# The chunked delta rule by pairs of heads instead of by chunks, in a two-model transformer kernel

## The chip, the cores and the metric

The kernel runs on one core of one Trainium2 chip. The metric is the device time of one launch in microseconds (us).

## The reference, cut to what matters

Two models run one after the other on 512 tokens of width 1024, each two layers deep, all in float32. The change touches only the mixer of the second model, which runs once in each of its two layers. One projection gives 19 ranges of 128 columns, and one of 286 that is kept by token. Nine of the 19 (q, k and v of six heads of width 64) pass a causal convolution of four taps and silu. Then comes the gated delta rule in chunks of 64 tokens:

```python
q = l2norm(q) * D ** -0.5;  k = l2norm(k)
g = jnp.cumsum(g, axis=-1)                       # inside each chunk of 64
decay = exp(where(incl, g[..., :, None] - g[..., None, :], -inf))
lower = where(strict, (k * beta) @ k.T * decay, 0)
u, w = split(triangular_solve(I + lower, [v * beta, k * beta * exp(g)]))
attn = q @ k.T * decay

def step(state, xs):                             # 8 steps, one a chunk
    v_new = u_i - w_i @ state
    o_i = (q_i * exp(g_i)) @ state + a_i @ v_new
    state = state * exp(g_last) + (k_i * exp(g_last - g_i)).T @ v_new
```

Seven further ranges (three of queries, four of keys and values of a sparse attention) are used by the attention that follows. Six of them are rotated by position first. The last three are the gate z of the delta rule.

## The kernel before

The second model's mixer, `second_mixer`, has two regions with a barrier of all engines between them. The first, in which the change lies, holds the norm of the input, the projection, the delta rule and the rotation. The second, `attention_region`, holds the attentions.

Within a region each helper (`items_lane`, `key_norm_lane`, `delta_lane`, `rotary_lane`) writes a program for every engine as a generator that yields planned times. `weave` sorts the programs of one engine by these times and issues them in that order. So the planned times fix nothing but the order of instructions on each engine. An engine that reaches a wait stops there with all that stands behind it.

The projection goes by items of 128 columns. One item is eight pieces of three matmuls (`three_products`, L493 to L495), as its operands are split in a high and a low half. Its weights are split by ScalarE (L479) and VectorE (L484) while three items of them fit in the buffers. A convolution item leaves its bank through one ScalarE copy (L765) and three VectorE operations (L794, L796, L798), then silu (L769). Four row items come first, then 19 of 128 columns: nine convolution items, three of z, three of queries, four of keys and values.

`key_norm_lane` normalises all six tiles of q and k when all convolution items are through. It starts with an explicit load of ScalarE's table set that holds both exp and ln, as `inverse_root` takes Ln (L549) and then Exp (L551).

`delta_lane` then makes four rounds, one for each 128 tokens. A round treats two chunks of 64 of all six heads. It computes decays (L3333, L3334), transposes k and v (L3336, L3338), and makes the two triangular matrices (`low`, `low_t`, L3495 to L3509 on VectorE). A block inverse takes five levels, each with a product L3373, a ScalarE copy L3466, products L3385 and L3390 and a VectorE subtraction L3524, twice over (`b` = 0, 1: the head of a pair). Then come u and w (L3399, L3404), two steps of the recurrence (L3417, L3422, L3429 on TensorE, L3535 and L3545 on VectorE) and the output (L3437, L3473, L3552). GpSimd makes masks and masked parts. Pieces of the last ten items are planned between these products.

`rotary_lane` is planned behind the last item: six products L3571, each with a GpSimd product (L3586) and two VectorE operations (L3595, L3598), then four products L3579 with copies L3605.

Of the kernel before, what the change touches and what calls it, by code (L numbers as in the profile page):

```python
# [17 lines left out]
P = 128  # L18
# [4 lines left out]
ALU = mybir.AluOpType  # L23
# [147 lines left out]
def second_constants():  # L171
# [5 lines left out]
    c["causal_row"] = np.concatenate([np.zeros((P, S - P)), causal], axis=1)  # L177
    c["strict_row"] = np.concatenate([np.where(i[None, :] <= i[:, None], NEG, 0.0), np.zeros((P, S - P))], axis=1)
# [442 lines left out]
class Item:  # L621


    def __init__(self, kind, load, at, width, out, chunks=(), scale=None, tile=0, func=None, moving=None, ready=(), each=()):
        self.kind, self.load, self.at, self.width, self.out = kind, load, at, width, out
        self.chunks, self.scale, self.tile, self.func, self.moving, self.ready, self.each = chunks, scale, tile, func, moving, ready, each
        self.begin, self.length = 0.0, 0.0
# [7 lines left out]
def items_lane(k, r, lane, w, ranges, items, h_ready, ring, w_hi, w_lo, banks, tap=None, bias=None, quick=False):  # L635
# [108 lines left out]
    def _(act):  # L744
        steps = [(split_time(part), 0, part) for part in range(len(parts))]
        for m, item in enumerate(items):
            end = item.begin + item.length
            if item.kind == "conv":
                steps += [(end, 2, m), (end + 3.0, 3, m)]
# [1999 lines left out]
def sparse_lane(k, r, lane, nq, ks2, kw2, vs_rows, vw_rows, cmp_out, gates, mixT, tile_out):  # L2749
# [67 lines left out]
    def _(dve):  # L2817
        def maxima(p):
            for u in range(2):
# [4 lines left out]
                nc.vector.tensor_tensor_reduce(probs[:, n % DEEP, 0:width(p)], logits[:, u, 0:width(p)], k.at["causal_row"][:, S - width(p):S],  # L2824
# [57 lines left out]
def stick_lane(k, r, lane, sq, sk, sv_rows, mixT, head_out, banks, out_ps, space, items_out, pairs_done, bank_free):  # L2882
# [62 lines left out]
    def _(dve):  # L2945
        def masked(n):
            for b in range(TC):
# [4 lines left out]
                nc.vector.tensor_tensor(z[:, n % 2, AT[b]:AT[b + 1]], banks[:, b % 2, 0:WIDTH[b]], k.at["strict_row"][:, 0:WIDTH[b]],  # L2952
# [102 lines left out]
def attention_region(k, a, l, tiles, nq, kc2, vc2, ks2, kw2, vs_rows, vw_rows, gates, sq, sk, sv_rows, gz, mixT):  # L3055
# [3 lines left out]
    with Region(k) as r:  # L3059
# [8 lines left out]
        kc_dup, vc_rows = r.sbuf("kc_dup", [P, 2 * N_CMP]), r.sbuf("vc_rows", [P, 2, HD])  # L3068

# [117 lines left out]
def key_norm_lane(k, r, lane, tiles, silu_done, sq, rstd, stat):  # L3187

    nc = k.nc
    (squared, stat_done, log_done, rstd_done, normed) = r.semaphores("qk", "squared stat_done log_done rstd_done normed")  # L3190
    N = len(tiles)

    @lane.vector
    def _(dve):
        for j in range(N + 1):
            yield j / (N + 1)
            if j < N:
                dve.wait_ge(silu_done, j + 1)
                if j >= 2:
                    dve.wait_ge(stat_done, j - 1)  # L3200
                nc.vector.tensor_tensor(sq[:, j % 2, :], tiles[j][0], tiles[j][0], ALU.mult).then_inc(squared, 1)
            yield (j + 0.5) / (N + 1)
            if j:
                x, scale = tiles[j - 1]
                dve.wait_ge(rstd_done, j)
                nc.vector.scalar_tensor_tensor(x, x, scale, rstd[:, (j - 1) % 2, :], ALU.mult, ALU.mult).then_inc(normed, 1)

    @lane.tensor
    def _(pe):
        for j in range(N):  # L3210
            yield (j + 0.1) / (N + 1)
            pe.wait_ge(squared, j + 1)
            if j >= 2:
                pe.wait_ge(rstd_done, j - 1)
            nc.tensor.matmul(stat[:, j % 2, :], k.at["ones_64"], sq[:, j % 2, :], start=True, stop=True).then_inc(stat_done, 1)

    @lane.scalar
    def _(act):
        nc.scalar.preload_act_table_set(EXP_LN_SET)
        for j in range(N):  # L3220
            yield (j + 0.5) / (N + 1)
            act.wait_ge(stat_done, j + 1)
            if j >= 2:
                act.wait_ge(normed, j - 1)
            inverse_root(k, act, rstd[:, j % 2, :], rstd[:, j % 2, :], stat[:, j % 2, :], 1.0, log_done, j + 1).then_inc(rstd_done, 1)

    return normed


def delta_lane(k, r, lane, qkv, g, beta, beta_eg, to_end, mixT, scratch, state, banks, steps_ready, normed, silu_done, ROUND):  # L3230

    nc = k.nc
    H, T, LEVELS = N_GDN, GDN_T, 5
    N = H * HD
    (zeroed, prepared, turn_done, decay_done, exp_done, run_done, rows_done, run_out, masked, tb_done, qrun_done, kk_done, kq_done,
     low_done, low_t_done, attn_done, first_done, inv_done, part_done, y_done, y_out, t_done, uw_done, uw_out, new_done, new_out,
     inter_done, grow_done, state_done, intra_done, inter_out, pass_out) = r.semaphores(
        "delta", "zeroed prepared turn_done decay_done exp_done run_done rows_done run_out masked tb_done qrun_done kk_done kq_done "
        "low_done low_t_done attn_done first_done inv_done part_done y_done y_out t_done uw_done uw_out new_done new_out "
        "inter_done grow_done state_done intra_done inter_out pass_out")  # L3240

    def pieces(first, count):
        return [scratch(first + i) for i in range(count)]

    def by_head(x):
        return x.rearrange("p (b t n) -> p b t n", b=2, t=T)

    v_beta, k_beta, k_end, q_run, run, attn_t, y_sb = pieces(0, 7)
    lows, invs = scratch(7, 2), scratch(9, 2)
    low, low_t = lows[:, 0:N], lows[:, N:2 * N]  # L3250
    inv, inv_t = invs[:, 0:N], invs[:, N:2 * N]
# [744 lines left out]
```

## Time and profile before

| what | us |
|---|---|
| median of three runs (lowest to highest) | 3831.06 (3827.61 to 3834.22) |
| the profiled execution, its own time | 3828.58 |
| its span | 3826.8 |
| TensorE busy in the span | 3475.4 (91%) |
| VectorE busy | 1780.1 (47%) |
| ScalarE busy | 1308.2 (34%) |
| GpSimd busy | 420.6 (11%) |
| mean granted TensorE clock | 0.949 of full |
| first region, layer 0, first convolution item to the last VectorE instruction | 1844.87 to 2094.1 |

A busy TensorE is not one at its peak: ends of matmuls are modelled, and a busy share holds stretches at the lower clock. The region stands in the trace twice, once for each layer, with nearly the same rows. Times of rows count from the start of the span.

### The profile page before, as it was taken

The page shows a single profiled execution, that of the slowest core. Times are in us where ns is not written, and L with a number is a line of the kernel's source. Part 1 is how long each engine was busy: PE and PEld are TensorE (multiplying, and loading weights), DVE is VectorE, ACT ScalarE, POOL GpSimd, SP SyncE. Part 2 cuts the span into 40 slices and gives each one's busy share as a digit, 9 for nine tenths or more (in the row PEclk, how much of TensorE's full clock was granted, in tenths as well). Part 3 has the DMA queues.
Part 4 walks back from the last instruction along what each step waited for, and adds up shares of the span by engine and source line. Part 5 has one row for each costly group of instructions (what it writes and reads, how often), then busy time and mean ns, then how long its engine had stood idle before and what let it go on. Part 6 is the DMA issues. An engine that isn't in the chain of part 4 may idle for free. (4 is left out here: it accounts for less than half of the span.)

```text
span 3826.8 us, 46458 instructions
## 1 busy us (share of the span) xinstructions
PE 3475.4 (91%) x19317; PEld 2705.3 (71%) x19317; DVE 1780.1 (47%) x2762; ACT 1308.2 (34%) x2038; POOL 420.6 (11%) x351
## 2 busy tenths in 40 slices
PE   5989897999999789998897988999989988899998
PEld 4877765788777567886665756788766665577886
DVE  4775465443332534332544454444444444554534
ACT  2332353223232332322422353333333134533333
POOL 0001000120000101100023000221001310013100
PEclk7999998999999899999899999999989989999999
DMA  6651215333221032331301103232122020213231
GB/s 228 199 175 45 78 34 187 118 124 110 90 75 55 1 132 69 105 109 35 99 18 27 37 1 110 87 100 101 66 76 61 2 63 1 88 55 110 77 110 50
DMA packets 230575, 316.69 MB, mean 83 GB/s; under 512 B 13133, under 2 KB 167606, under 8 KB 229086
## 3 DMA queue, kind: packets, MB, share of 16 engines
q1 hardware_dynamic: 230366, 313.72, 24.9%
q8 instruction: 154, 2.52, 0.3%
q14 instruction: 55, 0.45, 0.0%
HBM read 311.04 MB, written 6.85 MB: 83 GB/s over the span
## 5 line engine op out<-in xcount | busy, mean ns | idle before, releaser
L493 PE MATMUL out<-h_lo,w_hi 128*128 128x512 f32 x2608 | 1043.1, 400 | 52.1 <-DVE w_lo L484 47.8
L494 PE MATMUL out<-h_hi,w_hi 128*128 128x512 f32 x2608 | 1022.2, 392 | 0.0
L495 PE MATMUL out<-h_hi,w_lo 128*128 128x512 f32 x2608 | 1021.6, 392 | 0.0
L484 DVE TENSOR_TENSOR w_lo<-ring,w_hi 128x1024 fp32r<-128x1024 f32 (+2 forms) x459 | 560.7, 1227 | 980.0 <-ACT w_hi L479 974.9
L479 ACT ACTIVATE w_hi<-ring 128x1024 fp32r<-128x1024 f32 (+2 forms) x459 | 469.2, 1027 | 1152.9 <-PE out L495 1061.1
L493 PEld LDWEIGHTS out<-h_lo,w_hi 128*128 128x128 f32 x2608 | 494.0, 189 | 178.1 <-issue 60.4
L494 PEld LDWEIGHTS out<-h_hi,w_hi 128*128 128x128 f32 x2608 | 493.8, 189 | 111.9 <-issue 11.0
L495 PEld LDWEIGHTS out<-h_hi,w_lo 128*128 128x128 f32 x2608 | 493.6, 189 | 103.9
L493 PE MATMUL item_banks<-h_lo,w_hi 128*128 128x512 f32 (+1 forms) x632 | 289.4, 458 | 14.3 <-DVE w_lo L484 5.1
L494 PE MATMUL item_banks<-h_hi,w_hi 128*128 128x512 f32 (+1 forms) x632 | 255.1, 404 | 0.0
L495 PE MATMUL item_banks<-h_hi,w_lo 128*128 128x512 f32 (+1 forms) x632 | 254.8, 403 | 0.0
L493 PEld LDWEIGHTS item_banks<-h_lo,w_hi 128*128 128x128 f32 (+1 forms) x632 | 121.9, 193 | 55.4 <-issue 22.0
L493 PE MATMUL item_banks<-w_lo,h_hi 128*128 128x256 f32 (+1 forms) x320 | 104.7, 327 | 43.5 <-DVE w_lo L484 27.3
L495 PEld LDWEIGHTS item_banks<-h_hi,w_lo 128*128 128x128 f32 (+1 forms) x632 | 121.6, 192 | 31.0
L494 PEld LDWEIGHTS item_banks<-h_hi,w_hi 128*128 128x128 f32 (+1 forms) x632 | 122.4, 194 | 28.4 <-issue 8.2
L1503 POOL TENSOR_TENSOR tiles<-temp 128x512 f32<-128x512 f32 x44 | 72.8, 1655 | 568.8 <-DVE temp L1489 324.9
L428 DVE SCALAR_TENSOR_TENSOR tiles<-tiles,c_act 128x1024 f32<-128x1024 f32 x70 | 95.9, 1369 | 57.5 <-DMA tiles<-in_mod_w 56.3
L2264 POOL TENSOR_TENSOR tiles<-tiles 128x512 f32<-128x512 f32 x64 | 76.8, 1205 | 309.3 <-ACT tiles L2250 282.2
L1635 POOL TENSOR_TENSOR xT<-xT,tiles 128x512 f32<-128x512 f32 x20 | 30.2, 1537 | 709.8 <-DVE tiles L1624 709.8
L493 PEld LDWEIGHTS item_banks<-w_lo,h_hi 128*128 128x128 f32 x320 | 65.9, 206 | 57.7 <-DVE w_lo L484 27.9
L484 DVE TENSOR_TENSOR h_lo<-tiles,h_hi 128x2048 fp32r<-128x2048 f32 (+2 forms) x43 | 83.5, 1944 | 35.6 <-ACT h_hi L479 35.6
L494 PE MATMUL item_banks<-w_hi,h_hi 128*128 128x256 f32 (+1 forms) x320 | 96.8, 302 | 0.0
(499 smaller groups left out, 4635.8 us busy)
## 6 DMA issues: line engine op xcount, KB each, us to landing
ring<-in_mlp_w SPq DMA_DIRECT2D x30, 2048.0 KB, 8.5
ring<-in_w_up SPq DMA_DIRECT2D x44, 1024.0 KB, 7.4
tiles<-in_mod_w SPq DMA_DIRECT2D x80, 512.0 KB, 4.6
ring<-in_e_w_in SPq DMA_DIRECT2D x48, 512.0 KB, 4.1
ring<-in_w_down SPq DMA_DIRECT2D x10, 2048.0 KB, 7.7
ring<-in_w_in SPq DMA_DIRECT2D x16, 1024.0 KB, 5.2
ring<-in_o_w_in SPq DMA_DIRECT2D x7, 2048.0 KB, 7.9
tiles<-in_mod_w SPq DMA_DIRECT2D x8, 1024.0 KB, 8.8
```

Of the source, the lines that this page charges most:

```text
L428: nc.vector.scalar_tensor_tensor(total, slot, gain_of(c), total, ALU.mult, ALU.add).then_inc(summed, 1)
L479: return nc.scalar.activation(hi.bitcast(F32R), x, ACT.Copy)
L484: return nc.vector.tensor_tensor(lo.bitcast(F32R), x, hi, ALU.subtract)
L493: nc.tensor.matmul(out, wh, xl, start=start, stop=False, **kw)
L494: nc.tensor.matmul(out, wh, xh, start=False, stop=False, **kw)
L495: return nc.tensor.matmul(out, wl, xh, start=False, stop=stop, **kw)
L1503: nc.gpsimd.tensor_tensor(finish_dst(b.nth, j), acc[:, b.nth % 2, j, :], acc[:, b.nth % 2, 2 + j, :], ALU.mult).then_inc(finished, 1)
L1635: nc.gpsimd.tensor_tensor(k.xT[:, f, :], k.xT[:, f, :], temp[:, f, :], ALU.add).then_inc(pool_added, 1)
L2264: after=lambda j: nc.gpsimd.tensor_tensor(dst(j), dst(j), dst(j), ALU.mult))
```

## The change

The delta rule goes by pair of heads (three of them, `t`), with all four 128-token chunks at once. The tiles of one pair are 512 columns wide, where those of one round were 384 wide. The eight steps of the recurrence of pair t are planned beside the inverse of pair t+1. The states of all steps are kept (`hist`), so the products of q with the states are made together at the end of a pair. Items are reordered to q, k, v of pair 0, then pair 1, pair 2, then queries, keys and values, and z last. Each load of weights is now two transfers of 128 columns where it was one of 256. The silus of a pair stand together. The norms move into `delta_lane`, one pair at a time, and the explicit table load goes. The rotation stands behind the last item on the banks of the items, and waits for the output of pair 1. Two constants are merged into one, and three buffers of the attention are allocated later.

```diff
-        ranges += [[(W_GDN + t * 2 * P, 2 * P)] for t in range(2 * GDN_T)]
+        tile_of = [part * GDN_T + t for t in range(GDN_T) for part in range(3)]
+        cols_of = [W_GDN + j * P for j in tile_of] + [W_NQ + j * P for j in range(NSA_T)] + [W_KC, W_KC + P, W_KC + 2 * P, W_KW]
+        cols_of += [W_GDN + (3 * GDN_T + j) * P for j in range(GDN_T)]
+        ranges += [[(col, P) for col in cols_of[n:n + 2]] for n in range(0, len(cols_of), 2)]
...
-        BEGIN, DELTA, ROUND = 18.0, 94.0, 28.0
-            item.begin, item.length = at, 3.2 if item.load == 0 else 5.6 if at < DELTA else 9.4
+        BEGIN, PAIR, BESIDE = 18.0, 37.0, 7.0
+            item.begin, item.length = at, 3.2 if item.load == 0 else 5.6 if m < TC + 3 else BESIDE
+            items[TC + n].silu_at = last.begin + last.length + 2.0 + 0.7 * (n % 3)
+            here = items[TC + 2].silu_at + 8.5 + PAIR * t
+            pairs_at.append((here - 6.5 if t == 0 else here - 10.0, here, here + 36.0))
...
-        nc.scalar.preload_act_table_set(EXP_LN_SET)
...
+    def recurrence(pe, t, at):
...
+        for s in range(STEPS):
+            if s:
+                yield at + 2.6 * s
+                pe.wait_ge(state_done, (STEPS - 1) * t + s)
+                for b in range(2):
+                    last = nc.tensor.matmul((R0, R1)[b][rows, 0:HD], w_t[rows_of(b), (i * TC + c) * HD:(i * TC + c + 1) * HD], hist[rows_of(b), s, :],
+                                            start=True, stop=True)
+                last.then_inc(new_done, 1)
+            if s < STEPS - 1:
+                yield at + 2.6 * s + 1.3
+                if s:
+                    pe.wait_ge(new_out, (STEPS - 1) * t + s)
+                for b in range(2):
+                    last = nc.tensor.matmul(R0[rows_of(b), HD:2 * HD], of_head(k_end, b, c)[rows, :], of_head(u, b, c)[rows, :], start=True, stop=True)
+                last.then_inc(grow_done, 1)
...
+    def act_steps():
+            steps += [(norm_at + 1.3 + 1.3 * j, "norm", t, j) for j in range(2)]
+            steps += [(at + 1.5, "decay", t, 0), (at + 4.3, "run", t, 0), (at + 34.8, "uw", t, 0), (run_at + 2.6 * (STEPS - 1) + 1.6, "inter", t, 0)]
+            steps += [(at + 12.0 + 4.4 * n + 1.1 * b, "y", t, 2 * n + b) for n in range(LEVELS) for b in range(2)]
...
+    def dve_steps():
+            steps += [(at + 2.0, "rows", t, 0), (at + 4.2, "both", t, 0), (at + 6.0, "low", t, 0), (at + 8.5, "attn", t, 0)]
+            steps += [(at + 14.0 + 4.4 * n + 1.1 * b, "inv", t, 2 * n + b) for n in range(LEVELS) for b in range(2)]
+            steps += [(run_at + 2.6 * s + 0.7, "new", t, s) for s in range(1, STEPS)]
+            steps += [(run_at + 2.6 * s + 2.0, "state", t, s) for s in range(STEPS - 1)]
```

On TensorE a pair is planned as: decays at `at`, transposes +0.8, running sums +3.0, k times k (kk) +5.0, k times q (kq) +7.0, level n at +11.0 + 4.4n, u and w (uw) at +34.0.

## Rows read from the trace of the kernel before

**Rows 1.** The page's busy time of TensorE over the span.

```profile
PE 3475.4 (91%) x19317; PEld 2705.3 (71%) x19317; DVE 1780.1 (47%) x2762; ACT 1308.2 (34%) x2038; POOL 420.6 (11%) x351
```

**Rows 2.** Busy time by stretches of the first region, layer 0.

```profile
core 0: us, PE busy (x) PEld busy (x) DVE busy (x) ACT busy (x) POOL busy (x), PEclk, DMA share, GB/s
1845.00:1926.00 81.00, 74.43 (x290) 56.41 (x291) 44.95 (x58) 36.04 (x53) 4.67 (x5) 0.94 0.26 78
1926.00:1972.50 46.50, 43.46 (x625) 32.20 (x625) 19.41 (x39) 9.60 (x20) 13.21 (x15) 0.96 0.12 36
1972.50:2018.00 45.50, 42.63 (x620) 32.22 (x619) 17.73 (x37) 9.13 (x20) 13.18 (x15) 0.92 0.01 2
2059.20:2094.10 34.90, 27.87 (x554) 21.42 (x554) 15.79 (x36) 8.32 (x20) 9.75 (x11) 0.89 0.01 2
```

**Rows 3.** TensorE's waits, 1844 to 2037.4: us in total, times, longest.

```profile
PE delta_banks L3373 <- DVE delta_scratch L3509: 6.1, 3, 2.9
PE stat_banks L3215 <- DVE tiles L3201: 4.4, 2, 3.5
PE delta_banks L3333 <- DVE gdn_qkv L3206: 2.1, 1, 2.1
```

**Rows 4.** Timeline of TensorE, round 0: start, us, instructions.

```profile
1951.26 0.52 PE L3385 MATMUL delta_banks<-delta_scratch 64*64 64x64 f32 x12
1951.61 0.52 PE L3390 MATMUL delta_banks<-delta_scratch 64*64 64x64 f32 x12
...
1957.15 0.50 PE L493 MATMUL item_banks<-h_lo,w_hi 128*128 128x512 f32 x1
...
1958.05 0.56 PE L3373 MATMUL delta_banks<-delta_scratch,tiles 64*64 64x64 f32 x12
1958.54 0.50 PE L493 MATMUL item_banks<-h_lo,w_hi 128*128 128x512 f32 x1
```

**Rows 5.** Timeline of TensorE, items alone: two pieces in a row.

```profile
1855.13 0.40 PE L493 MATMUL item_banks<-h_lo,w_hi 128*128 128x512 f32 x1
...
1855.83 0.40 PE L493 MATMUL item_banks<-h_lo,w_hi 128*128 128x512 f32 x1
```

**Rows 6.** Timeline of VectorE: first and behind the last of the triangular block.

```profile
1936.78 0.61 DVE L3495 TENSOR_TENSOR delta_scratch<-delta_scratch,delta_banks 128x192 f32<-128x192 f32 x2
...
1940.90 0.61 DVE L3516 TENSOR_TENSOR delta_scratch<-delta_scratch,delta_banks 128x192 f32<-128x192 f32 x2
```

**Rows 7.** Timeline of VectorE at the end of a convolution item.

```profile
1898.05 0.75 DVE L794 SCALAR_TENSOR_TENSOR gdn_qkv<-item_banks,vec,gdn_qkv 128x511 f32<-128x511 f32 x1 [1.91 <-ACT gdn_qkv L765]
...
1900.51 1.22 DVE L484 TENSOR_TENSOR w_lo<-ring,w_hi 128x1024 fp32r<-128x1024 f32 x1
```

**Rows 8.** Timeline of ScalarE at the start of the norms.

```profile
1901.05 1.28 ACT L3219 ACT_TABLE_LOAD   x1
1903.56 0.69 ACT L549 ACTIVATE tiles<-stat_banks,const_sb 128x512 f32<-128x512 f32 x1 [1.22 <-PE stat_banks L3215]
```

**Rows 9.** Timeline of ScalarE in the first model: Exp, Ln, Exp.

```profile
122.64 1.28 ACT L844 ACT_TABLE_LOAD   x1
...
130.36 1.28 ACT L849 ACT_TABLE_LOAD   x1
131.65 0.26 ACT L849 ACTIVATE scan_scratch<-scan_scratch 128x64 f32<-128x64 f32 x1
131.93 1.28 ACT L853 ACT_TABLE_LOAD   x1
```

**Rows 10.** Timeline of TensorE: last item matmul, last two recurrence steps.

```profile
2037.07 0.40 PE L495 MATMUL item_banks<-h_hi,w_lo 128*128 128x512 f32 x1
...
2087.59 0.50 PE L3417 MATMUL delta_banks<-gdn_state,delta_scratch 64*64 64x64 f32 x9 [1.00 <-ACT delta_scratch L3470]
...
2088.87 0.56 PE L3429 MATMUL delta_banks<-delta_scratch 64*64 64x64 f32 x12 [0.37 <-DVE delta_scratch L3535]
2090.20 0.58 PE L3417 MATMUL delta_banks<-gdn_state,delta_scratch 64*64 64x64 f32 x6 [0.77 <-DVE gdn_state L3545]
```

**Rows 11.** Timeline of VectorE: a rotation's sum, and the region's last work.

```profile
2042.53 0.69 DVE L3598 TENSOR_TENSOR tiles<-tiles 128x512 f32<-128x512 f32 x1 [0.73 <-POOL tiles L3586]
...
2093.50 0.62 DVE L3552 TENSOR_TENSOR tiles<-tiles,delta_banks 128x192 f32<-128x192 f32 x2
```

More of the change, by code:

```diff
@@ L748, in _ @@
             if item.kind == "conv":
-                steps += [(end, 2, m), (end + 3.0, 3, m)]
+                steps += [(end, 2, m), (end + 3.0 if item.silu_at is None else item.silu_at, 3, m)]
             elif owner(m) == "act":
@@ L3193, in _ @@
     @lane.vector
     def _(dve):
[L3195 to L3218, printed above, removed]
-        nc.scalar.preload_act_table_set(EXP_LN_SET)
[L3220 to L3225, printed above, removed]
@@ L3633, in second_mixer @@
+        ranges += [[(col, P) for col in cols_of[n:n + 2]] for n in range(0, len(cols_of), 2)]
         items = [Item("rows", 0, 0, 2 * P + 30, by_token[:, c:c + 1, :], (c,)) for c in range(TC)]
-        items += [Item("conv", 1 + j // 2, j % 2 * P, P, qkv[:, j, :], tile=j) for j in range(3 * GDN_T)]
-        items += [Item("feat", 1 + j // 2, j % 2 * P, P, gz[:, j - 3 * GDN_T, :]) for j in range(3 * GDN_T, 4 * GDN_T)]
-        items += [Item("feat", 7 + j // 2, j % 2 * P, P, nq[:, j, :], scale=HD ** -0.5) for j in range(NSA_T)]
@@ L3637, in second_mixer @@
-        items += [Item("feat", 8, P, P, kv[:, 0, :]), Item("feat", 9, 0, P, kv[:, 1, :]), Item("feat", 9, P, P, kv[:, 2, :]),
-                  Item("feat", 10, 0, P, kv[:, 3, :])]
-        last_kv = len(items)
-        BEGIN, DELTA, ROUND = 18.0, 94.0, 28.0
+        outs = [qkv[:, j, :] for j in tile_of] + [nq[:, j, :] for j in range(NSA_T)] + [kv[:, j, :] for j in range(4)] + [gz[:, j, :] for j in range(GDN_T)]
+        last_kv = TC + 3 * GDN_T + NSA_T + 4
+        for n, out in enumerate(outs):
+            if n < 3 * GDN_T:
+                items.append(Item("conv", 1 + n // 2, n % 2 * P, P, out, tile=n))
+            else:
+                items.append(Item("feat", 1 + n // 2, n % 2 * P, P, out, scale=HD ** -0.5 if n < 3 * GDN_T + NSA_T else None))
@@ L3641, in second_mixer @@
+        BEGIN, PAIR, BESIDE = 18.0, 37.0, 7.0
         at = BEGIN
-        for item in items:
-            item.begin, item.length = at, 3.2 if item.load == 0 else 5.6 if at < DELTA else 9.4
+        for m, item in enumerate(items):
+            item.begin, item.length = at, 3.2 if item.load == 0 else 5.6 if m < TC + 3 else BESIDE
             at += item.length
+        for n in range(3 * GDN_T):
+            last = items[TC + 3 * (n // 3) + 2]
+            items[TC + n].silu_at = last.begin + last.length + 2.0 + 0.7 * (n % 3)
@@ L3646, in second_mixer @@
+        pairs_at = []
+        for t in range(GDN_T):
+            here = items[TC + 2].silu_at + 8.5 + PAIR * t
+            pairs_at.append((here - 6.5 if t == 0 else here - 10.0, here, here + 36.0))
         with mixing as r:
-            scratch_own = r.sbuf("delta_scratch", [P, 11 * N_GDN * HD])
+            scratch_own = r.sbuf("delta_scratch", [P, 12 * S])
             scratch_mix = mixT[:, GDN_T:DT, :].rearrange("p f n -> p (f n)")
-            state = r.sbuf("gdn_state", [P, GDN_T, HD])
+            hist, ends = r.sbuf("gdn_hist", [P, 2 * TC, HD]), r.sbuf("gdn_ends", [P, 2, 2 * TC])
@@ L3655, in scratch @@
             def scratch(first, count=1):
-                width = N_GDN * HD
-                if first < 11:
-                    return scratch_own[:, first * width:(first + count) * width]
-                return scratch_mix[:, (first - 11) * width:(first - 11 + count) * width]
+                if first < 12:
+                    return scratch_own[:, first * S:(first + count) * S]
+                return scratch_mix[:, (first - 12) * S:(first - 12 + count) * S]
             tables = r.lane(30.0, 0.0)
```

688 lines of the change are left out of this document (363 added, 325 removed).

## The prediction

> **What bounds the kernel now.** I read the page first. TensorE is busy in 91% of the span [rows 1]. So what another engine saves is worth only what TensorE waits for it. The change lies in one region, which stands in the trace twice, and I read its stretches next. In layer 0 it runs from the first convolution item at 1844.87 to the last VectorE work at 2094.1, so 249.2 us. TensorE is nearly full there until the last item ends, and less so at the end: 27.9 of the last 34.9 us [rows 2].
>
> The region splits at the last item matmul, which ends near 2037.4 [rows 10]. The first part takes 192.5 us and the tail 56.7 us. For the first part I rebuild the sum from prices. A piece of an item takes 0.70 us when pieces follow each other [rows 5], so 19 items of eight pieces are 106.4. Twelve small delta records start 0.35 us behind the twelve before them [rows 4]. A round has 528 such records, at most 15.4 us by this price, and some 3 us of wide products. By their starts in the same view a round is 17 us. Two and a half rounds lie before the last item ends, 42.2. Six norm products are 5.1. Next comes a cost of switching. A piece that stands alone between delta groups takes 0.90 us, and a lone group of twelve 0.49 [rows 4]. So each change from items to delta work and back costs 0.20 + 0.14 = 0.34 us. The timeline has 46 such pieces or runs of pieces, 15.6 us. The waits are 13.0: three for the triangular block, two in the norms, one in front of the first round, and 0.4 of others [rows 3]. The granted clock was 0.94, 0.96 and 0.92 in three stretches [rows 2], each a mean of time at 2.4 GHz and some at 1.2 GHz, which loses 4.9 + 1.9 + 3.6 = 10.4. The sum is 192.7, against 192.5 measured. So this account can be used on the changed order.
>
> **The content does not change.** Five levels of four rounds of three pairs are five levels of three pairs of four chunks. Only six products for each of the first or last steps fall away. The same matmuls, masks and copies are done in wider pieces. VectorE and ScalarE save some fixed time, but neither is the bound [rows 1]. What changes is order.
>
> **The tail, a gain.** After the last item the changed TensorE program has one level and a half, u and w of pair 2, one recurrence and the whole rotation. A recurrence step now lasts 1.28 + 1.33 us without cover [rows 10], with 24 and 12 records and several VectorE operations in it. The changed step has four records and one VectorE operation on either side. Nothing shows it, so I bound it: it can't be longer than 2.6, and two lone matmuls of 0.27 us with two VectorE operations of about 0.3 give 1.15 at least. I take 1.3, near the lower end: seven steps, 9.1. The rotation stands beside them. A sum of it waits 0.73 us on VectorE for GpSimd's product [rows 11], and what stands behind it in VectorE's order, the recurrence's steps too, waits as well. Walking the orders from the last item gives 7 us to u and w, 4 to the first step, 13 for the steps with rotation between them (the 9.1, and 4 for four of its products at 1.0), and 3 for the outputs, 27. At 2.6 a step it would be 36. TensorE is half idle there. The clock stood at 0.89 in the present tail [rows 2], so I add 3. That makes 30 where 56.7 stood: 26.7 less.
>
> **The first part, work that moves in.** The tail keeps 280 small records (8.2 us) and the ten products of the rotation. All other delta work, 68 (four rounds) less 8.2, now lies before the last item ends, with items and norms 171.3 in all. It was 153.7, so 17.6 more.
>
> **Switching, a loss.** I sort the planned times of the diff. Sixteen items stand beside the pairs, one piece each 0.875 planned microseconds. A level has four groups spread over 4.4, and new and grow steps of the recurrence stand alone between them. So 84 groups of delta work stand between pieces where 46 stood. 38 more at 0.34 are 12.9 us.
>
> **Waits.** These I walk through, each from the place in the orders.
> - The triangular block held VectorE from 1936.78 to 1940.90, 4.1 us for 384 columns [rows 6]. For 512 it is 5.3. In pairs 1 and 2 the `low` step (at + 6.0) stands in VectorE's order 0.2 before the state of step 2 of the recurrence beside it. TensorE's next `new` product needs this state, and only two pieces, 1.6 us, stand between. So TensorE stands for 3.8 us, twice. Queued behind are kq and all items. Smaller ones of this kind (rows, weight splits and copies ahead of `new`) are 1.5 + 0.3 + 0.6. In pair 0 no recurrence stands beside it, and nine pieces cover the block: 0.6.
> - The end of a convolution item holds VectorE for three operations and a weight split, 1898.05 to 1901.7 [rows 7], 3.6 us. Before, all nine stood ahead of the delta rule. Now six stand beside pair 0. Nearly all are covered by two or three pieces, but the last stands in front of the subtraction that u and w need: 1.8.
> - The norms. The explicit load of ln with exp goes [rows 8]. In the first model, where none stands between, Exp, Ln and Exp each bring a load of 1.28 us [rows 9]. So each norm now brings a load for Ln and one for Exp, 12 a layer, and the silus of pairs 1 and 2 bring three more, where one stood: 14 more, 18 us of ScalarE. Most are hidden. In pair 0 the two norms take 6.5 us instead of 4, the next item's convolution sits on VectorE before the second, and the transposes of k wait 4.5 us where 0.7 would do. In pair 1 the loads add 1.0 in front of u and w, in pair 2 0.3.
>
> The sum is 7.6 + 2.4 + 0.6 + 1.8 + 4.5 + 1.3 = 18.2, against 13.0: 5.2 more. Three stand for about 4 us, and the present stretches with such waits lost 2 to 4 us of clock each [rows 2, 3]. I take 11 against 10.4.
>
> A row shows the load at 1.28 us with the next activation right behind it [rows 9]. The Trainium skill (ScalarE: Activation LUTs, What ACT_TABLE_LOAD costs) gives the same 1283 ns, but adds a drain of some 1380 ns to every switch, and its section on table sets says to batch calls by set, which speaks against this change. By that price the three waits at norms would be some 5 us a layer longer. The row shows no drain, so I leave it out.
>
> **At no cost.** The weights now come in two transfers of 128 columns. Each is asked for some three items (17 us) ahead of its use. Doubled transfers would have to take three times as long to show. GpSimd's wider masks run a level ahead. The merged constant and moved buffers cost nothing.
>
> **Sum.** For one layer 17.6 + 12.9 + 5.2 + 0.6 - 26.7 = 9.6 us more, for two 19. The profiled execution took 3828.6, 2.5 below the median, which is 3831.1. So 3850, and 0.5% slower. Own range of this case: switching 26 to 32, waits 14 to 24, clock 8 to 14, tail 28 to 36 a layer, not all at one end: 3838 to 3866.
>
> **Rivals.**
> - *Faster: TensorE doesn't stop.* If VectorE has the small recurrence steps through before the triangular block, and the norms keep ahead, waits are 5 instead of 18.2, and the clock loses 3 instead of 11. That is 21.2 less a layer: 11.6 faster than now, so 3808. Waits plus clock below 19.6 us a layer decide it. For it speaks that more pieces stand between the stages than now. Against it speaks that the block's place is fixed in the order. Chance 0.24.
> - *Even: the loads don't bite.* One set chosen for Ln and Exp, or norms that are early, take away 4.7 of waits and 2.5 of clock a layer: 2.4 slower a layer, 3836. Rows 9 speak against it. Chance 0.20.
> - *Much slower: the fine steps don't fit.* Beside levels, each of 28 recurrence hops waits another 0.4 us, as VectorE and ScalarE are caught by splits of weights: 11.2 more a layer, 3873. TensorE's present waits in steps are only 0.4 to 1.0 [rows 10], without cover. Chance 0.06.
>
> **Numbers.** The forecast's case has 0.50. What a measurement of this kernel can tell from no change is 0.2%, 7.7 us. Faster by more: 0.25, most of it the first rival. Within: 0.20. Slower: 0.55. Leaving out a tenth on each side, the range reaches from just above the first rival's value to the last one's: 3811 to 3868.
>
> **What would show it.** The last item matmul of layer 0 should end near 2074 to 2077 (content 171.3, switching 28.6, waits 18.2, clock 11 from 1844.87), and the region near 2104. The waits of TensorE should name the VectorE product into `hist` at 3 to 4 us, twice a layer, and the transposes of k in pair 0. ScalarE should have 14 more table loads a layer. Lone pieces should still take 0.90. I am wrong if the last item ends before 2065, if loads are few, or if the tail is over 40 us.

## The result, and the profile after

The changed kernel takes 3850.98 us, median of five runs (3847.08 to 3857.33), against 3831.06 before. The ratio is 1.0052, with a 95% interval of 1.0038 to 1.0066. The forecast was 3850, and "slower" its likeliest side. The sum came out right; two of its parts did not, and they cancelled.

The profiled run was the slowest of the five, 3857.3. At the first convolution item of layer 0 it was already 5.2 us behind (1850.11 against 1844.87), so I compare lengths from there. The page's busy times first:

```profile
PE 3511.2 (91%) x19257; PEld 2707.5 (70%) x19257; DVE 1779.7 (46%) x2718; ACT 1338.2 (35%) x2040; POOL 420.9 (11%) x309
```

They hardly differ from [rows 1]: 36 us more of TensorE and 30 of ScalarE, each about a hundredth of the span. What changed can be read only by place. Busy time by stretches of the changed region in layer 0, to be held against [rows 2]; its last item ends at 2072.1 and the next region's first product stands at 2109.6:

```profile
1850.00:1900.00 50.00, 48.78 (x285) 36.62 (x285) 34.01 (x47) 28.06 (x42) 15.87 (x12) 0.97 0.33 85
1900.00:1950.00 50.00, 46.33 (x587) 33.39 (x587) 23.18 (x31) 23.54 (x34) 8.36 (x8) 0.97 0.17 44
1950.00:2000.00 50.00, 46.33 (x632) 33.32 (x630) 22.28 (x39) 9.81 (x17) 16.43 (x12) 0.97 0.13 33
2000.00:2072.10 72.10, 65.37 (x801) 45.51 (x799) 26.62 (x47) 17.46 (x28) 13.53 (x9) 0.95 0.01 2
...
2072.10:2088.00 15.90, 13.68 (x233) 8.33 (x232) 10.28 (x18) 2.84 (x6) 8.85 (x6) 1.00 0.00 1
2088.00:2109.60 21.60, 16.67 (x116) 8.67 (x116) 4.39 (x15) 2.98 (x5) 0.00 (x0) 0.51 0.00 1
```

The reader is to see two things in the seventh column, the granted clock. In the first part it is 0.95 to 0.97, no worse than before. In the tail it is 1.00 up to 2088 and then 0.51, which is 1.2 GHz nearly throughout. Where it fell, TensorE runs a recurrence step, waits, and runs the next. That these waits bring the clock down is not shown by this row.

From the first convolution item to the last item's end the kernel before took 192.6 us in layer 0 and 189.6 in layer 1; after, 222.0 and 222.2. From there to the next region's first product it took 57.9 and 57.7, and now 37.5 and 37.4. So layer 0 loses 9.0 and layer 1 loses 12.3. The 3 us between them are the old kernel's: its first part lost 10.0 us to the clock in layer 0 and 6.8 in layer 1 (length times what the mean granted clock lacks to 1), with the same order and the same stops.

TensorE's waits in the first part of layer 0 (us in total, times, longest), which answer to [rows 3]:

```profile
PE stat_banks L3412 <- DVE gdn_hist L3582: 9.0, 2, 5.3
PE delta_banks L3381 <- ACT delta_scratch L3482: 4.0, 2, 2.6
PE item_banks L492 <- DVE w_lo L483: 2.6, 1, 2.6
PE delta_banks L3364 <- DVE delta_scratch L3563: 1.0, 1, 1.0
PE delta_banks L3325 <- DVE gdn_qkv L3518: 0.8, 1, 0.8
PE stat_banks L3313 <- DVE tiles L3514: 0.3, 1, 0.3
```

The first row is the predicted stop: the product `new` waits for the state in `hist`, once beside pair 1 (3.7 us) and once beside pair 2 (5.3). The third row stands ahead of the first convolution item, in both kernels. Without it the waits are 15.1; by the same count they were 13.1 before.

The timeline of VectorE shows the first of these stops from the inside:

```profile
1957.10 0.75 DVE L3538 TENSOR_TENSOR delta_scratch<-delta_scratch,delta_banks 128x256 f32<-128x256 f32 x2 [1.26 <-PE delta_banks L3343]
1957.77 0.75 DVE L3542 TENSOR_TENSOR delta_scratch<-delta_scratch,delta_banks 128x256 f32<-128x256 f32 x2
1958.55 1.75 DVE L3546 TENSOR_TENSOR delta_scratch<-delta_scratch,const_sb 128x1024 f32<-128x1024 f32 x1
1960.40 2.10 DVE L3549 TENSOR_TENSOR delta_scratch<-const_sb,delta_scratch 128x1024 f32<-128x1024 f32 x1
1962.42 0.27 DVE L3582 SCALAR_TENSOR_TENSOR gdn_hist<-gdn_hist,gdn_ends,stat_banks 128x64 f32<-128x64 f32 x1
```

And TensorE's timeline on the other side:

```profile
1957.85 0.33 PE L3420 MATMUL stat_banks<-delta_scratch,gdn_qkv 64*64 64x64 f32 x4
...
1962.74 0.37 PE L3412 MATMUL stat_banks<-gdn_hist,delta_scratch 64*64 64x64 f32 x2 [3.67 <-DVE gdn_hist L3582]
```

The operation that TensorE needs is 0.27 us long and could have started at 1958.2. It stands behind 5.3 us of the triangular block.

The second row of waits was not predicted at that place. ScalarE's timeline behind it:

```profile
1931.57 0.37 ACT L3482 ACTIVATE delta_scratch<-delta_banks 128x256 f32<-128x256 f32 x1
1931.95 1.28 ACT L548 ACT_TABLE_LOAD   x1
1933.24 0.69 ACT L548 ACTIVATE tiles<-stat_banks,const_sb 128x512 f32<-128x512 f32 x1
1933.95 1.28 ACT L550 ACT_TABLE_LOAD   x1
1935.24 0.63 ACT L550 ACTIVATE tiles<-tiles 128x512 f32<-128x512 f32 x1
1935.78 0.67 ACT L764 ACTIVATE gdn_qkv<-item_banks,vec 128x512 f32<-128x512 f32 x1
1936.35 1.05 ACT L478 ACTIVATE w_hi<-ring 128x1024 fp32r<-128x1024 f32 x1
1937.30 0.37 ACT L3482 ACTIVATE delta_scratch<-delta_banks 128x256 f32<-128x256 f32 x1
```

Between two copies of the last level stand one norm of the next pair with two table loads, a convolution's first tap and a weight split: 5.4 us. The region has 17 loads where it had 3, the 14 more that were forecast.

In the tail, TensorE's timeline: first a product of the rotation at the high clock with what follows it, then the recurrence of the last pair. The rotation has six products L3608 and four L3616, all of the same size.

```profile
2073.60 1.13 PE L3608 MATMUL item_banks<-tiles,const_sb 128*128 128x512 f32 x2
2074.65 0.68 PE L3376 MATMUL delta_banks<-delta_scratch 64*64 64x64 f32 x16
...
2086.12 0.33 PE L3412 MATMUL stat_banks<-gdn_hist,delta_scratch 64*64 64x64 f32 x4 [0.75 <-DVE gdn_hist L3582]
2086.84 0.33 PE L3420 MATMUL stat_banks<-delta_scratch,gdn_qkv 64*64 64x64 f32 x4 [0.39 <-DVE delta_scratch L3572]
...
2096.49 0.48 PE L3412 MATMUL stat_banks<-gdn_hist,delta_scratch 64*64 64x64 f32 x4
2097.35 0.48 PE L3420 MATMUL stat_banks<-delta_scratch,gdn_qkv 64*64 64x64 f32 x4 [0.38 <-DVE delta_scratch L3572]
2097.76 2.07 PE L3616 MATMUL item_banks<-tiles,const_sb 128*128 128x512 f32 x2
2099.76 0.48 PE L3412 MATMUL stat_banks<-gdn_hist,delta_scratch 64*64 64x64 f32 x4
```

I call it a hop from one product of four records, over VectorE's answer, to the next. A hop is 0.72 us at the high clock (2086.12 to 2086.84) and 0.86 at the low one (2096.49 to 2097.35). A product of the rotation costs 2.00 at the low clock (2097.76 to 2099.76) and 1.06 at the high one (2073.60 to 2074.65).

### The profile page after: what moved, and what is told of

Same layout as the page of the kernel before. It is cut to its first block and busy times, and to the rows that moved or that the text cites. A ratio compares the mean times of both kernels' runs of the same rounds, so it can differ in the third digit from the quotient of the medians.

```text
span 3855.6 us, 46228 instructions
## 1 busy us (share of the span) xinstructions
PE 3511.2 (91%) x19257; PEld 2707.5 (70%) x19257; DVE 1779.7 (46%) x2718; ACT 1338.2 (35%) x2040; POOL 420.9 (11%) x309
## 5 line engine op out<-in xcount | busy, mean ns | idle before, releaser
L492 PE MATMUL item_banks<-h_lo,w_hi 128*128 128x512 f32 (+1 forms) x632 | 299.6, 474 | 14.1 <-DVE w_lo L483 5.1
L492 PEld LDWEIGHTS item_banks<-h_lo,w_hi 128*128 128x128 f32 (+1 forms) x632 | 123.0, 195 | 57.7 <-issue 22.1
```

Of the source, the lines that this page charges most:

```text
L492: nc.tensor.matmul(out, wh, xl, start=start, stop=False, **kw)
```

## The experiments

In the code of an experiment a diff is against the changed kernel, if nothing else is said. The measured lengths are those of layer 0, layer 1 behind a stroke: first part (first convolution item to the end of the last) and tail (from there to the next region's first product). They come from one profiled execution of each kernel, the ratios from all that were timed. "Stops" are gaps of TensorE over 0.2 us in layer 0's first part, "groups" the groups of delta work that stand between pieces there. A ratio moves by a thousandth for 3.8 us, and its interval reaches 0.9 to 1.4 thousandths either way.

| kernel | ratio to before (95%) | first part | tail | stops | groups |
|---|---|---|---|---|---|
| before | 1 | 192.6 / 189.6 | 57.9 / 57.7 | 13.1 | 54 |
| changed | 1.0052 (1.0038 to 1.0066) | 222.0 / 222.2 | 37.5 / 37.4 | 15.1 | 90 |
| set | 1.0034 (1.0022 to 1.0047) | 218.7 / 217.4 | 37.6 / 37.6 | 12.2 | 90 |
| block in three | 1.0039 (1.0025 to 1.0053) | 219.4 / 218.1 | 37.6 / 37.6 | 13.9 | 90 |
| block in four | 1.0002 (0.9993 to 1.0011) | 214.5 / 214.6 | 34.0 / 33.9 | 9.5 | 90 |
| pieces in twos | 1.0004 (0.9995 to 1.0013) | 213.8 / 211.7 | 36.4 / 37.6 | 14.3 | 57 |
| items of 7.6 | 1.0079 (1.0065 to 1.0092) | 231.1 / 229.9 | 32.0 / 32.0 | 16.9 | 91 |
| no rotation | not measured | 222.0 / 223.8 | 26.0 / 25.4 | as changed | 90 |
| three edits | 0.9932 (0.9919 to 0.9944) | 198.9 / 197.6 | 37.6 / 37.6 | 4.8 | 57 |
| the same, in fours | 0.9932 (0.9919 to 0.9945) | 197.7 / 198.0 | 39.7 / 39.6 | 8.2 | 32 |
| the same, items of 6.6 | 0.9948 (0.9935 to 0.9962) | 199.6 / 198.3 | 40.4 / 40.9 | 10.4 | 55 |
| the same, items of 7.4 | 0.9976 (0.9968 to 0.9985) | 209.2 / 207.9 | 36.4 / 36.4 | 9.9 | 56 |
| the same, rotation early | 0.9919 (0.9906 to 0.9933) | 199.0 / 197.6 | 36.1 / 36.1 | 4.8 | 57 |
| before, in twos | 1.0022 (1.0012 to 1.0032) | 193.6 / 190.7 | 59.5 / 59.5 | 16.7 | 38 |

**The set.** Are the table loads in a place that counts?

```diff
+                if n == 0:
+                    nc.scalar.preload_act_table_set(EXP_LN_SET)
                 inverse_root(k, act, rstd[:, n, :], ...
...
```

> The changed kernel with one line more: ScalarE loads the set that holds ln and exp once ahead of each pair's two norms, so that Ln and Exp don't bring a load each. The changed kernel stands at 1.0052 of the one before. Theory (the loads are late in places that count: 2.65 and 1.37 us of TensorE's waits in front of the last level of pairs 0 and 1, 0.8 at the transposes of k, and about 2 us of clock behind them, a layer): 12 us less in all, a ratio near 1.002, table loads down from 58 to about 40, and these waits under 1 us. Rival (ScalarE is at 35%, the loads only fill its idle time, and the waits are those of the norms themselves): ratio 1.004 to 1.006 with as many fewer loads.

The loads fell from 58 to 40, and the two waits for ScalarE's copies (4.0 us) are gone. But 0.8 us came back in front of u and w and 0.4 at the transposes. The time is 1.8 thousandths lower, some 7 us of the 12 expected. The two intervals overlap, but the first part is shorter in both layers, by 3.3 and 4.8 us. So the loads do bite. The edit takes away nine of the 14 further loads a layer, and what the other five cost is not measured.

**The block in three.** Does VectorE's order make the stops at the state?

The block's six operations stay in their order, and stand under three names instead of one:

```diff
-            steps += [(at + 2.0, "rows", t, 0), (at + 4.2, "both", t, 0), (at + 6.0, "low", t, 0), (at + 8.5, "attn", t, 0)]
+            steps += [(at + 2.0, "rows", t, 0), (at + 4.2, "both", t, 0), (at + 6.0, "low_t", t, 0), (at + 6.3, "low", t, 0), (at + 7.6, "first", t, 0), (at + 8.5, "attn", t, 0)]
...
```

> The changed kernel with VectorE's triangular block in three steps instead of one (products for the transposed half, products for the other half, then the first level's two wide operations), so that the state and the new value of steps 2 and 3 of the recurrence beside it get in between. The same operations. Theory (VectorE's order makes the 3.67 and 5.29 us stalls of pairs 1 and 2): both fall below 1.5 us, with 2 us of clock that is 9 to 10 us a layer, 19 in all, a ratio near 1.000. Rival (the block is the chain itself: what doesn't wait at the recurrence waits at the first level for the block's end): the wait goes to the first level or to the product with the new value, and the ratio stays at 1.003 or above.

The gain is 1.3 thousandths, a quarter of the theory's, and the intervals overlap, so it is hardly clear of noise. The rows tell more. In pair 2 the stop of 5.3 became two of 0.7 and 1.6. In pair 1 it grew from 3.7 to 1.8 + 3.8. VectorE's timeline there says why:

```profile
1954.33 2.09 DVE L483 TENSOR_TENSOR w_lo<-ring,w_hi 128x1024 fp32r<-128x1024 f32 x1 [1.51 <-ACT w_hi L478]
1956.45 0.29 DVE L3574 TENSOR_TENSOR delta_scratch<-delta_scratch,stat_banks 64x128 f32<-64x128 f32 x1
1956.77 1.86 DVE L3548 TENSOR_TENSOR delta_scratch<-delta_scratch,const_sb 128x1024 f32<-128x1024 f32 x1
1958.74 2.10 DVE L3551 TENSOR_TENSOR delta_scratch<-const_sb,delta_scratch 128x1024 f32<-128x1024 f32 x1
1960.87 0.75 DVE L3558 TENSOR_TENSOR delta_scratch<-delta_scratch,delta_banks 128x256 f32<-128x256 f32 x2
1961.54 0.27 DVE L3584 SCALAR_TENSOR_TENSOR gdn_hist<-gdn_hist,gdn_ends,stat_banks 128x64 f32<-128x64 f32 x1
```

The new value now waits behind a weight split, and the state of the next step behind both wide operations. The stop had only moved one step on. That pointed to a cut between the wide ones.

**Pieces in twos.** Is the 0.34 us per change from items to delta work real?

```diff
-                    yield item.begin + item.length * f / DT
+                    yield item.begin + item.length * (f - f % item.group) / DT
...
+            item.group = 1 if m < TC + 3 else 2
```

> The changed kernel with the items' pieces planned in twos beside the delta rule, so that 55 groups of delta work a layer stand between pieces instead of 86. The same work on all engines. Theory (each change from items to delta work and back costs TensorE 0.34 us): 31 x 0.34 = 10.5 us a layer less, 2 of it lost again as groups get less fine cover, so 17 less in all, a ratio near 1.001; two pieces in a row should take 1.60 us where two lone ones take 1.80. Rival (the extra time of a lone piece is time in which TensorE would wait for the other engines anyway): the waits in front of the levels grow by as much, and the ratio is 1.004 or above.

4.8 thousandths, with 33 groups fewer and stops as before. The timeline shows two pieces, the first and the group behind the second, 1.58 us apart, where two lone ones take 1.80:

```profile
1910.09 0.50 PE L492 MATMUL item_banks<-h_lo,w_hi 128*128 128x512 f32 x1
...
1911.67 0.68 PE L3376 MATMUL delta_banks<-delta_scratch 64*64 64x64 f32 x16
```

In layer 0 the first part is 8.2 us shorter. Stops give 0.8 of it, and the clock took 2.2 (from its rows, 10.3 us lost against 8.1). So 9.6 us go to 33 groups, 0.29 each. In layer 1 the same sum gives 0.25. The rival, that this time would be waited anyway, falls.

**Items of 7.6.** Would cover for the last level shorten the tail?

```diff
-        BEGIN, PAIR, BESIDE = 18.0, 37.0, 7.0
+        BEGIN, PAIR, BESIDE = 18.0, 37.0, 7.6
```

> The changed kernel with one number changed: an item beside the pairs is planned for 7.6 instead of 7.0, so that the 16 items reach to the last recurrence, and only it and the rotation stand behind the last item. Theory (the tail of 36 us is long because the last level, u and w and the recurrence stand there without cover, at half clock): the tail falls to about 24 us, the first part grows by 4.4 of content and 1 of switching, 6 to 7 us a layer less, a ratio near 1.002. Rival (pieces planned further apart leave the earlier hops with less cover): the first part's waits grow by 6 us a layer or more, and the ratio is 1.005 or above.

The rival's time came out, and not its mechanism: the first part grew by 9.1 and the tail fell by 5.5 only, but stops grew by 1.8 where the rival wanted 6. What moved in is 206 small records (1762 against 1968 stand in the first part), 6.0 us at the price of [rows 4], where I had put 4.4. With the stops and a group more that is 8.1 of the 9.1. My 24 us for it was wrong: the last recurrence, with all ten products of the rotation beside it, takes 32 by itself, however much cover the last level has.

**Three edits**, the first and third of these, and the block cut in four:

```diff
-            steps += [(at + 2.0, "rows", t, 0), (at + 4.2, "both", t, 0), (at + 6.0, "low", t, 0), (at + 8.5, "attn", t, 0)]
+            steps += [(at + 2.0, "rows", t, 0), (at + 4.2, "both", t, 0), (at + 6.0, "low_t", t, 0), (at + 6.3, "low", t, 0), (at + 7.6, "first", t, 0), (at + 8.9, "minus", t, 0),
+                      (at + 9.0, "attn", t, 0)]
...
```

> Three edits together: pieces in twos, the ln and exp set loaded once a pair, and VectorE's triangular block in four steps, with the state of step 3 between its two wide operations. Theory (the gains are of different kinds and add up: the twos alone gave 4.8 thousandths, the set 1.8; and the block gives more than the 1.3 thousandths of the cut in three, as no more than 2 us of it now stand in front of a state): 0.9965, about 13 us under the kernel before. Rival (the split of w_lo, which stands in VectorE's order beside the block, takes the place of each wait taken away): 0.999 to 1.001, with the wait named on w_lo's neighbour, the new value.

Better than both kernels, and better than its own theory. The block cut alone, below, says where the theory was short: it gives 5.0 thousandths, and the theory had left about 2 for it. Its stretches, to be held against those above (its items end at 2044.0):

```profile
1845.00:1900.00 55.00, 53.78 (x376) 41.34 (x377) 38.07 (x50) 25.98 (x42) 19.90 (x14) 0.97 0.30 77
1900.00:1950.00 50.00, 48.55 (x616) 35.30 (x614) 26.63 (x41) 20.32 (x32) 10.21 (x9) 1.00 0.17 44
1950.00:2000.00 50.00, 48.77 (x714) 37.46 (x715) 21.28 (x35) 13.88 (x24) 12.35 (x9) 1.00 0.13 33
2000.00:2044.00 44.00, 42.88 (x597) 32.13 (x597) 19.32 (x38) 6.84 (x14) 12.01 (x8) 1.00 0.01 2
2044.00:2081.60 37.60, 30.40 (x348) 17.07 (x349) 14.66 (x32) 5.82 (x11) 8.89 (x7) 0.71 0.00 1
```

From 1900 on the clock is 1.00 as long as items last. The stops at the state are 1.4 us in place of 9.0, and VectorE's timeline shows the state between the wide operations:

```profile
1950.10 1.86 DVE L3551 TENSOR_TENSOR delta_scratch<-delta_scratch,const_sb 128x1024 f32<-128x1024 f32 x1
1951.98 0.28 DVE L3588 SCALAR_TENSOR_TENSOR gdn_hist<-gdn_hist,gdn_ends,stat_banks 128x64 f32<-128x64 f32 x1
1952.18 1.98 DVE L3555 TENSOR_TENSOR delta_scratch<-const_sb,delta_scratch 128x1024 f32<-128x1024 f32 x1
```

**The block in four alone**, to see whether it needs the other two:

> The changed kernel with nothing but VectorE's triangular block cut in four steps, the state of step 3 standing between its two wide operations. Theory (in the kernel with three edits the stops at the state fell from 9.0 to 1.4 us a layer, by this edit; what the twos add there is small): stops at the state and the new value under 4 us, the clock of 1950 to 2000 above 0.98, 8 to 10 us a layer less, ratio near 1.0005. Rival (the three edits work only together: with lone pieces a split of w_lo takes the place of the block again, as in the cut in three, 5.6 us in pair 1): ratio 1.003 or above.

It doesn't. The wait at the state fell to 1.6 us (1.8 more at the new value), and the ratio by 5.0 thousandths. With 1.8 for the set and 4.8 for the twos the single edits make 11.6, and together they measured 12.0. So each of the three pays without the others. One thing was off: the clock of 1950 to 2000 stayed at 0.97, and ScalarE's stops of 4.0 us are still there; it rose to 1.00 only behind 2000.

By place they add up less neatly. In the first part of layer 0 the single edits take 3.3, 8.2 and 7.5 us, 19.0 together, where the three at once take 23.1. The rest of the block's gain, 3.5 us a layer, stands in the tail, which TensorE runs in the same order as before the edit:

```profile
2056.90:2090.80 33.90, 26.73 (x348) 15.57 (x349) 14.66 (x32) 5.82 (x11) 8.84 (x7) 0.85 0.00 1
```

It has 0.85 of the clock there where the changed kernel has 0.72. With the three edits the tail is back at 37.6 us and 0.71. What sets the clock of the tail is not shown, and this profiled execution was 4.9 us below its kernel's median, so part of these 3.5 may be the execution and not the edit.

**In fours.**

```diff
-            item.group = 1 if m < TC + 3 else 2
+            item.group = 1 if m < TC + 3 else 4
```

> As the kernel with three edits, with the pieces in fours: 29 groups of delta work by the plan instead of 55. Theory (TensorE pays per change, by the step from ones to twos 0.22 to 0.29 us): 26 x 0.25 = 6.5 us a layer less than in twos, minus what waits grow; if these grow by 3, 0.9945. Rival (groups in fours leave hops of levels back to back, each waiting 0.5 to 1 us for ScalarE's or VectorE's answer, 20 of them and more): waits grow by 10 us a layer or more, and it is slower than in twos, 0.998 or above.

Neither came out: the ratio is that of twos. In layer 0 the first part is 1.2 us shorter. 48 small records (1.4 us) moved from it to the tail, stops grow by 3.4 and the clock takes 1.7 more, so 25 groups fewer bring about 5 us, 0.20 each. The tail takes 2.1 back. From twos to fours the two prices balance.

**Items of 6.6 and of 7.4** with the three edits:

> As the kernel with three edits, with 6.6 instead of 7.0 for an item: the items end 6.4 planned us earlier, and another level and a half stand in the tail, beside the rotation's products. Theory (7.6 instead of 7.0 moved 4.4 us of content and the cover of the rotation, and cost 9 in the first part for 5.5 in the tail; the rotation's products are better filler beside levels than beside the small steps at half clock): the first part 6 to 8 us shorter, the tail 4 longer, 2 to 4 us a layer less than with 7.0. Rival (levels without cover pay 0.5 to 1 us a hop at half clock): the tail grows by 8 or more, no gain or slower.

> As the kernel with three edits, with 7.4 instead of 7.0 for an item: the items reach to u and w of the last pair, and only the last recurrence, its outputs and the rotation stand behind. Theory (7.6 cost more than it gave because the first part grew by 9 where 4.4 moved in; the rest of it were switching and stops, which the three edits have made cheap): first part 5 to 6 longer, tail 5 shorter, within 0.1% of 7.0, 0.993. Rival (the tail is bound by the last recurrence and the rotation beside it, so that cover given to the last level is cover taken from nothing): slower by 3 us a layer or more, 0.9947 or above.

Both slower, the first by little: its interval overlaps that of 7.0, and its two parts together are 3.4 and 4.0 us longer a layer. With 6.6 a stop of 5.1 us stands in front of pair 0's first level. In VectorE's order a convolution item's three operations and a weight split (1893.74 to 1898.5) have come between the two wide operations that the cut had parted. At 7.0 no such stop is there. Taken off by subtraction it would leave 6.6 ahead by 1 to 2 us a layer; no run shows that. So this run tells of a collision, and leaves its theory open. With 7.4 the first part grows by 10.3, of which 5.1 are stops and 3.7 the 128 small records that moved in, and the tail falls by 1.2. Cover given to the last level brings almost nothing.

**No rotation.** The call of the rotation's lane is left out. What is the tail made of?

> The changed kernel without the rotation of q and k and its ten products (the outputs differ for that): it shows the tail of the last recurrence alone. By the forecast's working (a step 1.3 us, the rotation adds 4 in the steps and some 6 before them) the tail, 37.5 us from the last item to the next region's first product, would fall by about 10, and a step would be 1.3. Theory now (the tail is long because TensorE is at 1.2 GHz from 2088 on, and each rotation product costs 2.0 there and 1.06 before): it falls by 14 or more, and steps stay at 1.73 us. Rival (the chain of the recurrence bounds it, the rotation is hidden): it falls by less than 5.

The tail fell by 11.5 us in layer 0 and 12.0 in layer 1, halfway between the forecast's own working (10) and the theory (14 or more). By parts neither held: 3.2 us went before the first step and 8.3 in the steps, where the forecast had 6 and 4. The steps stay at 1.73 us, for which the forecast had 1.3. TensorE's timeline at the change of clock:

```profile
2080.76 0.33 PE L3412 MATMUL stat_banks<-gdn_hist,delta_scratch 64*64 64x64 f32 x4 [0.37 <-DVE gdn_hist L3582]
2081.48 0.48 PE L3420 MATMUL stat_banks<-delta_scratch,gdn_qkv 64*64 64x64 f32 x4 [0.39 <-DVE delta_scratch L3572]
2082.35 0.48 PE L3412 MATMUL stat_banks<-gdn_hist,delta_scratch 64*64 64x64 f32 x4 [0.38 <-DVE gdn_hist L3582]
```

A hop is 0.72 at the high clock (2080.76 to 2081.48) and 0.86 from 2082.35 on, with nothing beside it: two hops, a step, are some 1.43 or 1.73.

**Rotation early**, the three edits and one number:

```diff
-            rotary_lane(k, r, r.lane(at + 1.0, 24.0), ...
+            rotary_lane(k, r, r.lane(at + 1.0, 14.0), ...
```

> As the kernel with three edits, with the rotation's lane 14 instead of 24 planned us long: its ten products stand among the last level, u and w and the first two steps of the recurrence. Theory (the four turning products cost 2.00 us each at 1.2 GHz, and 1.06 at 2.4; standing earlier, while the clock is still high, they save 3 to 4 us, and the steps behind them are bare at 1.73): 2 to 4 us a layer less, 0.9915. Rival (the clock falls as soon as TensorE has idle time in the steps, and each step left bare waits for VectorE where now a product stands): the tail as long or longer, 0.993 or above.

The tail is 1.5 us shorter, at a clock of 0.81 instead of 0.71, but a product L3616 of the rotation (L3622 in this kernel) now waits 2.4 us for a sum on VectorE. The median is 3799.91 against 3805.34, and the intervals overlap: no more than a hint of 0.1%.

**The kernel before, in twos.** Would the old order have had the same gain? The diff is against the kernel before:

```diff
-                    yield item.begin + item.length * f / DT
+                    yield item.begin + item.length * (f - f % item.group) / DT
...
+            item.group = 1 if at < DELTA else 2
```

> The kernel before, with the pieces of the items beside its rounds in twos. It shows what that edit is worth without the change. Theory (the price per switch is the same there, and there are fewer to save: 54 groups, some 20 less in twos): 20 x 0.25 = 5 us a layer, 0.9975, and the hops of the chunk rounds, six heads wide, keep their cover. Rival (a round is dense, its hops need a piece each, and pieces in twos leave every second hop bare): the waits in front of the levels grow by 5 us a layer or more, 1.000 or above.

No, it gets slower by 2.2 thousandths. 16 groups fewer, but 3.6 us more of stops, and a tail 1.6 to 1.8 us longer. New waits there:

```profile
PE delta_banks L3417 <- ACT delta_scratch L3470: 1.0, 1, 1.0
PE delta_banks L3373 <- DVE delta_scratch L3524: 0.9, 3, 0.4
PE delta_banks L3399 <- DVE delta_scratch L3527: 0.5, 1, 0.5
```

Beside the chunk rounds seven items are planned (and not ten, as I wrote of the kernel before; in the trace 7.6 stand behind the first delta product), beside the pairs sixteen. That the changed order gains because it has more pieces to group is my reading, and no run varies their number alone.

## Why the prediction was right, and where it was not

- **The sum.** Forecast +9.6 us a layer; measured +9.0 and +12.3. Forecast 229 to 232 for the first part (2074 to 2077 counted from 1844.87); measured 222, which is 2066.9 by that count, 2 us above the 2065 that I had named as a sign of being wrong. Forecast 30 for the tail up to VectorE's last work, 26.7 less than before; measured 36.3 (2072.1 to 2108.4), 20.4 less. The first part was 7 too high and the tail 6 too low. The right total is in part luck.
- **Content, +17.6.** Not varied by a run, but the trace counts it. The first part has 1762 small records where it had 1250. At 0.35 us for twelve these are 14.9 us more, and the wide products of one round more are some 1.6: 16.5. In the tail 326 records stand, for which I had 280.
- **Switching, +12.9.** The count was 84 and is 90, against 54 instead of 46. As a residue the price is 0.31 after the change (222.0 less 171.3, 15.1 of stops and 8.1 of clock leaves 27.5 for 90 groups) and 0.29 before it. A residue takes up what is wrong in the other terms, and with the three edits it is 0.37. Differences between runs give 0.29 and 0.25 (ones to twos) and 0.20 (twos to fours). So 36 groups more are some 7 to 11 us. The twos showed that it is a cost and not covered time. The step holds, too dear.
- **Waits, 18.2.** They are 15.1. The largest term, the block ahead of the state, was forecast at 7.6 and is 9.0, at exactly that place; the cut in four took most of it away. The norms' loads were forecast at 4.5 for the transposes of k and 1.3 for u and w. They are 0.8 and nothing; instead they stop the last level by 4.0, since ScalarE runs its order and the norms of the next pair stand between copies of this one. Right count, nearly the right size, wrong place. The 1.8 at u and w and the 2.4 of small ones did not appear.
- **Clock, 11.** By the rows it is 8.1, less than the 10.4 before and not more.
- **The tail.** This is the mis-sized term. Up to the first step it took 11.9 us for 11 forecast, the outputs 4.2 for 3. The steps with the rotation between them were forecast at 13, with 3 of clock for the whole tail. They take 20.2 us (2083.98 to 2104.18). I had taken 1.3 a step from two VectorE operations of 0.3 and two products of 0.27; what TensorE waits between is 0.38 to 0.39 at each hop, and a step is 1.43. Bare and nearly all at the low clock the seven steps take 11.9 (no rotation), so the rotation adds 8.3 where I had 4. The rest is the clock: 21.6 us at 0.51, where I had assumed the 0.89 of [rows 2]. Four products of the rotation at 2.00 in place of 1.06 are 3.8 us of it. With the block cut alone the same order had 0.85 of the clock, and its steps took 16.6. The 36 that I had named as the upper bound met the number, but by another way: it stood for bare steps of 2.6, which no run shows.
- **The first rival, faster at 3808.** It asked for waits plus clock under 19.6; they are 23.2. With the three edits they are 4.8 + 1.7, and the kernel takes 3805. That is near the rival's value, but with fewer groups as well, which the rival had left alone. So waits and clock were two of the things that decide, and the switching was another.
- **The even rival, 3836.** The nine loads taken away bite by 7 us in all, half of its 14.
- **Transfers and GpSimd at no cost.** TensorE's waits name neither a transfer nor GpSimd in the first part.

The Trainium skill (ScalarE: Activation LUTs, What ACT_TABLE_LOAD costs) gives a drain of some 1380 ns beside the load. The trace disagrees: the load at 1931.95 starts 0.01 us behind the copy's end, and the activation at 1933.24 starts 0.01 us behind the load's. The advice of the Trainium skill (ScalarE: Activation LUTs, Table sets: the hidden batching unit) to batch calls by set agrees with the run of the set: 58 loads became 40 and the ratio fell by 1.8 thousandths.

## What to carry to other kernels

A small operation that TensorE needs must not stand behind a wide block in another engine's order; cut the block and put it between, and look where the next step of the chain then stands, since a cut at the wrong place only moves the stop. Interleaving has a price for each change of kind, here 0.2 to 0.3 us, and a gain in cover; the right grain depends on how much filler there is, and what is right for one order (twos here) is wrong for another (the kernel before). When work is moved out of a tail, size what stays by its bare chain, at the high and at the low clock, and not by the mean clock of the tail that it replaces. Here one order of TensorE's tail ran at 0.72 and at 0.85 of the clock, 3.5 us apart.

## What I had not expected of the hardware

- Hops between TensorE and VectorE, four records and one operation of 0.28 us, took 0.72 us at the high clock and 0.86 at the low one. The low clock costs such a chain 20%, but a product of 512 columns nearly twice (1.06 to 2.00).
- A norm with its two table loads, a tap and a weight split between two copies stopped TensorE for 2.6 us, although ScalarE is busy in 35% of the span.
- Fewer stops went with more clock: in the kernel with the three edits, with 4.8 us of them instead of 15.1, the clock stood at 1.00 from 1900 to 2044, where 0.97 and 0.95 had been granted. That the stops alone did it is not shown: the kernel before lost 10.0 us of clock in layer 0 and 6.8 in layer 1 with the same stops.
